# The opening stage of a two-layer diffusion transformer step: token array loaded first, one modulation chunk in halves, constants moved in the queue, dummy products added

## The reference

```
m = silu(cond) @ w_ada + b_ada           -> shift1, scale1, gate1, shift2, scale2, gate2
h = rms_norm(x, g_mix) * (1 + scale1) + shift1
q, k, v, gb, gc, xin = split(h @ w_in)   # k, q of the latent tokens get rotary positions (cos, sin)
x = x + gate1 * (concat(diff_attention(q, k, v), gb * short_conv(gc * xin)) @ w_out)
h = rms_norm(x, g_ffn) * (1 + scale2) + shift2
x = x + gate2 * ffn(h)                   # layer 0: SwiGLU; layer 1: the best 2 of 8 experts
```

## Time and profile before

| | |
|---|---|
| median of 3 runs | 2062.04 us (2062.03 to 2066.11) |
| the profiled execution | 2062.37 us |
| its span, first to last instruction | 2060.6 us |
| mean granted TensorE clock | 0.962 |
| busy: PE, DVE, ACT, POOL | 93%, 52%, 39%, 6% |

### The profile page before, as it was taken

The page is one execution under the profiler, slowest core; times in us unless marked ns, Lnnn a source line. Parts: engine busy times, 40 slices in busy tenths (PEclk is TensorE's granted clock), DMA queues, the critical chain, the costliest instruction groups (busy, mean ns, idle before and its releaser), DMA issues. The chain is left out here.

```text
span 2060.6 us, 29699 instructions
## 1 busy us (share of the span) xinstructions
PE 1915.9 (93%) x12189; PEld 1737.4 (84%) x12189; DVE 1067.3 (52%) x1661; ACT 799.6 (39%) x1278; POOL 113.4 (6%) x93
## 2 busy tenths in 40 slices
PE   4699988999999999989999898699999999999795
PEld 2699957989999999989997687689898898988784
DVE  1542576443232322336326754577686676866574
ACT  3321155242211222233213643455565565655552
POOL 2000000100000000110000001020000000002201
PEclk7899999989999999989999999799999999999997
DMA  8314300322322242304251010467666676668551
GB/s 318 133 72 184 122 12 1 123 93 93 133 72 103 108 168 72 113 31 159 88 199 58 1 42 33 169 218 232 216 225 223 218 231 218 221 225 296 172 174 52
DMA packets 84813, 289.53 MB, mean 141 GB/s; under 512 B 10660, under 2 KB 14116, under 8 KB 84672
## 3 DMA queue, kind: packets, MB, share of 16 engines
q1 hardware_dynamic: 78192, 270.14, 37.7%
q0 software_dynamic: 6480, 17.43, 2.5%
HBM read 281.12 MB, written 12.26 MB: 142 GB/s over the span
## 5 line engine op out<-in xcount | busy, mean ns | idle before, releaser
L1502 DVE TENSOR_TENSOR w_lo<-raw,w_hi 128x1024 fp32r<-128x1024 f32 x396 | 490.7, 1241 | 433.0 <-ACT w_hi L1084 419.7
L1084 ACT ACTIVATE w_hi<-raw 128x1024 fp32r<-128x1024 f32 x396 | 417.6, 1055 | 377.6 <-PE ps L615 179.3
L615 PE MATMUL ps<-a_hi,w_hi 128*128 128x320 f32 x1728 | 402.6, 315 | 32.6 <-DVE w_lo L1502 15.9
L615 PE MATMUL ps<-a_lo,w_hi 128*128 128x320 f32 x1728 | 397.5, 312 | 0.0
L615 PE MATMUL ps<-a_hi,w_lo 128*128 128x320 f32 x1728 | 397.3, 311 | 0.0
L928 PE MATMUL ps<-hg,w_hi 128*128 128x416 f32 x1232 | 384.5, 370 | 12.8 <-DVE w_lo L1502 10.7
L615 PEld LDWEIGHTS ps<-a_hi,w_hi 128*128 128x128 f32 x1728 | 291.5, 191 | 50.6 <-issue 30.6
L929 PE MATMUL ps<-hg,w_lo 128*128 128x208 f32 x1232 | 317.4, 258 | 0.0
L615 PEld LDWEIGHTS ps<-a_lo,w_hi 128*128 128x128 f32 x1728 | 292.6, 190 | 0.0
L615 PEld LDWEIGHTS ps<-a_hi,w_lo 128*128 128x128 f32 x1728 | 292.4, 190 | 0.0
L928 PEld LDWEIGHTS ps<-hg,w_hi 128*128 128x128 f32 x1232 | 234.3, 190 | 15.3 <-DVE w_lo L1502 11.2
(11 more groups left out here) (212 smaller groups left out, 2039.2 us busy)
## 6 DMA issues: line engine op xcount, KB each, us to landing
raw<-gu_w SPq DMA_DIRECT2D x222, 512.0 KB
raw<-moe_down_w SPq DMA_DIRECT2D x88, 512.0 KB
ada_raw<-ada_w SPq DMA_DIRECT2D x21, 2048.0 KB, 8.0
raw<-in_w SPq DMA_DIRECT2D x48, 512.0 KB
raw<-down_w SPq DMA_DIRECT2D x22, 512.0 KB
raw<-out_w SPq DMA_DIRECT2D x16, 512.0 KB
ada_pro<-ada_w SPq DMA_DIRECT2D x3, 2048.0 KB, 17.5
y_rows<-ey POOLq DMA_DIRECT2D x7, 512.0 KB, 3.6
```

Source lines behind the costliest of these rows:

```text
L615: ins = nc.tensor.matmul(out[:, hf, 0:HALF], w, o[:, hf * HALF:(hf + 1) * HALF], start=f, stop=e)
L1084: nc.scalar.activation(w_hi[:, s, :], raw[:, n % RAW, :], ACT.Copy).then_inc(hi_done, 1)
L1502: nc.vector.tensor_tensor(w_lo[:, s, :], raw[:, n % RAW, :], w_hi[:, s, :].bitcast(F32), ALU.subtract)\
```

## The change

ADA_FIRST and the blocks are written in another order, KEEP_BUSY gives a number of dummy products ahead of each item, the loads are issued in another order, the last opening chunk comes in two halves of columns with a semaphore each, DVE's wait for the late constants moves to the first rotary step, and the lambda sums and token numbers move behind chunk v0, with a semaphore of their own for lam_qk.

```diff
-ADA_FIRST = [("rows", 0, 0), ("rows", 0, 1), ("rows", 1, 0), ("turn", 0, 0), ("norm", 0, 0), ("rows", 1, 1),
-             ("spread", 0, 0), ("turn", 1, 0)]
+ADA_FIRST = [("rows", 0, 0), ("norm", 0, 0), ("rows", 0, 1), ("spread", 0, 0), ("rows", 1, 0), ("turn", 0, 0),
+             ("rows", 1, 1), ("turn", 1, 0)]
+KEEP_BUSY = {("rows", 0, 0): 40, ("norm", 0, 0): 4, ("rows", 0, 1): 2, ("spread", 0, 0): 0, ("rows", 1, 0): 8,
+             ("turn", 0, 0): 0, ("rows", 1, 1): 2, ("turn", 1, 0): 2}
             # SP
-            sp.dma_start(ada_raw[:], quad(0, 0, 0)).then_inc(ada_full, 16)
             for dst, src in ((bada, b_ada), (idn, ident), (gmix, g_mix)):
                 sp.dma_start(dst[:], src).then_inc(consts_in, 16)
             for kb in range(KB):
                 sp.dma_start(x[:, kb, :], xT[:, kb, :]).then_inc(x_in[kb], 16)
-                if kb == KB // 2 - 1:
-                    sp.dma_start(ada_pro[:, 0], quad(0, 0, 1)).then_inc(pro_full[0], 16)
-            for q in range(2):
-                sp.dma_start(ada_pro[:, 1 + q], quad(0, 1, q)).then_inc(pro_full[1 + q], 16)
+            sp.dma_start(ada_raw[:], quad(0, 0, 0)).then_inc(ada_full, 16)
+            sp.dma_start(ada_pro[:, 0], quad(0, 0, 1)).then_inc(pro_full[0], 16)
+            sp.dma_start(ada_pro[:, 1], quad(0, 1, 0)).then_inc(pro_full[1], 16)
+            for hf in range(2):
+                cols = slice(512 * hf, 512 * (hf + 1))
+                sp.dma_start(ada_pro[:, 2, :, cols], quad(0, 1, 1)[:, :, cols]).then_inc(pro_full[2 + hf], 16)
...
                 for item, c in IN_ITEMS[l][0]:
+                    if c == 2 and l == 0:
+                        for dst, src in late:
+                            sp.dma_start(dst[:], src).then_inc(late_in, 16)
                     if c == RAW:
                         if l == 0:
                             sp.wait_ge(mm_done, ROWS_FIRST[-1] + 1)
-                            for dst, src in late:
-                                sp.dma_start(dst[:], src).then_inc(late_in, 16)
+                            sp.dma_start(lq, lam_qk.partition_broadcast(P)).then_inc(lam_in, 16)
             # PE
+            def keep_busy(g, count):
+                for _ in range(count):
+                    nc.tensor.matmul(ps[:, g % 4, 1, 0:P], ones[:], ones[:], start=True, stop=True)
...
                 for hf in range(2):
+                    if arrived:
+                        pe.wait_ge(arrived[hf], 16)
                     for j in range(QUAD):
...
+                    if arrived and hf == 0:
+                        ins.then_inc(half_rows, 1)
             # ACT
                     for kb in range(KB):
-                        if kb == KB // 2:
-                            act.wait_ge(mm_done, ROWS_FIRST[1] + 1)
-                            take_rows(0, g0)
                         square(0, kb)
                     root(0, D)
+                    act.wait_ge(mm_done, ROWS_FIRST[1] + 1)
+                    take_rows(0, g0)
+                    act.wait_ge(mm_done, q0 + ADA_FIRST.index(("turn", 0, 0)) + 1)
+                    act.wait_ge(half_rows, 1)
+                    take_half_rows(1, g0, 0)
                     act.wait_ge(mm_done, ROWS_FIRST[3] + 1)
-                    act.wait_ge(mm_done, q0 + ADA_FIRST.index(("turn", 0, 0)) + 1)
-                    take_rows(1, g0)
+                    take_half_rows(1, g0, 1)
             # DVE
+                    reciprocal_root(0)
                     dve.wait_ge(row_done, 1)
                     dve.sem_inc(blk_free, 1)
                     modulation(l, 0, g0 + ADA_BLOCK["turn", 0], q0 + ADA_FIRST.index(("turn", 0, 0)))
-                    reciprocal_root(0)
-                    dve.wait_ge(row_done, 2)
-                    dve.sem_inc(blk_free, 1)
-                    modulation(l, 1, g0 + ADA_BLOCK["turn", 1], q0 + ADA_FIRST.index(("turn", 1, 0)))
-                    split_lo(0)
-                    split_lo(1)
-                norm(2 * l, operand[l, "h1"])
-                if l == 0:
-                    dve.wait_ge(late_in, 16 * 10)
-                    for each in range(LAYERS):
-                        lambda_sums(each)
-                    token_numbers()
+                    def first_gains():
+                        dve.wait_ge(row_done, 3)
+                        dve.sem_inc(blk_free, 1)
+                        split_lo(0)
+                        modulation(0, 1, AT[0, "ada"][2] + ADA_BLOCK["turn", 1],
+                                   AT[0, "ada"][1] + ADA_FIRST.index(("turn", 1, 0)), 1)
+                        split_lo(1)
+                norm(2 * l, operand[l, "h1"], first_gains if l == 0 else None)   # called behind the second st
...
+                        if (l, kind, j) == (0, "k", 0):
+                            dve.wait_ge(late_in, 16 * 9)
...
                         dve.wait_ge(vt_ready, 4 * l + j + 1)
                         dve.sem_inc(blk_free, 1)
+                        if l == 0 and j == 0:
+                            dve.wait_ge(lam_in, 16)
+                            for each in range(LAYERS):
+                                lambda_sums(each)
+                            token_numbers()
```

More of the change, by code:

```diff
@@ L118 @@
     LO_BASE.append(LO_BASE[-1] + 2 + FB + (ST if _e == LAST_E else 0))
-ADA_FIRST = [("rows", 0, 0), ("rows", 0, 1), ("rows", 1, 0), ("turn", 0, 0), ("norm", 0, 0), ("rows", 1, 1),
-             ("spread", 0, 0), ("turn", 1, 0)]
-ADA_BLOCK = {("rows", 0): 0, ("rows", 1): 1, ("turn", 0): 2, ("turn", 1): 3, ("norm", 0): 4, ("spread", 0): 4}
+ADA_FIRST = [("rows", 0, 0), ("norm", 0, 0), ("rows", 0, 1), ("spread", 0, 0), ("rows", 1, 0), ("turn", 0, 0),
+             ("rows", 1, 1), ("turn", 1, 0)]
+ADA_BLOCK = {("rows", 0): 1, ("rows", 1): 2, ("turn", 0): 3, ("turn", 1): 3, ("norm", 0): 4, ("spread", 0): 4}
 QUAD = 4
+KEEP_BUSY = {("rows", 0, 0): 40, ("norm", 0, 0): 4, ("rows", 0, 1): 2, ("spread", 0, 0): 0, ("rows", 1, 0): 8,
+             ("turn", 0, 0): 0, ("rows", 1, 1): 2, ("turn", 1, 0): 2}
 def mingle(items, groups, allowed):
@@ L394, in hybrid_step @@
         ada_full = sem("ada_full")
-        pro_full = [sem(f"pro_full{i}") for i in range(3)]
+        pro_full = [sem(f"pro_full{i}") for i in range(4)]
         cs_ready = sem("cs_ready")
@@ L646, in norm_sums @@
                 n0, q0, g0 = NORM_AT[i]
-                open_block(g0)
+                if i:
+                    open_block(g0)
                 pe.wait_ge(ss_add, KB * (i + 1))
@@ L653, in norm_spread, with weigh_conditions @@
                 spread(NORM_AT[i][2], diag[:].rearrange("p t c -> p (t c)"))
-            def weigh_conditions(src, g, q, first, last):
+            def weigh_conditions(src, g, q, first, last, arrived=()):
                 for hf in range(2):
+                    if arrived:
+                        pe.wait_ge(arrived[hf], 16)
                     for j in range(QUAD):
@@ L667, in turn_rows @@
                 for j in range(KB):
-                    ins = nc.tensor.matmul(ps[:, g % 4, 0, 2 * j:2 * j + 2], mrow[:, j * P:(j + 1) * P], fold[:],
+                    if halves and j == KB // 2:
+                        pe.wait_ge(row_done, count + 1)
+                    ins = nc.tensor.matmul(ps[:, g % 4, int(halves), 2 * j:2 * j + 2], mrow[:, j * P:(j + 1) * P], fold[:],
                                            start=True, stop=True)
@@ L692, in _ @@
                     for kind, grp, q in ADA_FIRST:
+                        spread_done = (kind, grp, q) in ADA_FIRST[ADA_FIRST.index(("spread", 0, 0)) + 1:]
+                        keep_busy(g0 + ADA_BLOCK["turn" if spread_done else "norm", 0], KEEP_BUSY[kind, grp, q])
                         g = g0 + ADA_BLOCK[kind, grp]
@@ L696, in _ @@
                             weigh_conditions(ada_raw, g, q, True, False)
+                        elif (kind, grp, q) == ("rows", 1, 1):
+                            weigh_conditions(ada_pro[:, 2], g, q, False, True, pro_full[2:])
                         elif kind == "rows":
@@ L719, in _ @@
                         if item[1] == "turn":
-                            turn_rows(g0 + b, item[2] + 1)
+                            turn_rows(g0 + b, item[2] + 2)
                         else:
@@ L851, in _ @@
                             if item[1] == "turn":
-                                turn_rows(g, item[2] + 1)
+                                turn_rows(g, item[2] + 2)
                             else:
@@ L1127, in take_rows, with take_half_rows @@
                                      ps[:, (g0 + ADA_BLOCK["rows", grp]) % 4, :, :], ACT.Copy).then_inc(row_done, 1)
+            def take_half_rows(grp, g0, hf):
+                nc.scalar.activation(mrow[:, 512 * hf:512 * (hf + 1)],
+                                     ps[:, (g0 + ADA_BLOCK["rows", grp]) % 4, hf, :], ACT.Copy).then_inc(row_done, 1)
             act.wait_ge(cond_in, 16)
@@ L1519, in halves, with norm @@
                 return a.rearrange("p (a b) -> p a b", a=2)
```

(4 more changed lines are left out.)

14 lines of the change are left out of this document (8 added, 6 removed).

## The result

The changed kernel took 2043.35 us (median of 4 runs, 2041.94 to 2047.64) against 2064.07 us (4 runs, 2062.03 to 2066.69) of the kernel before: ratio 0.9901, 95% interval 0.9885 to 0.9917, so 20.7 us faster. The profiled execution took 2042.01 us, 20.4 less than that of before. Forecast were 26.2 less for it and 2036.0 for the median, with 2041.5 as the range's upper end: the direction and the gain at k2 are right, the gain in the opening is half of what was forecast.

What follows compares the result with a forecast made beforehand. The prediction took PE, busy 93%, as the bound, with time to give only where it idles or slows: 2062.37 (profiled) - 15.9 - 2.4 - 7.9 = 2036.2, median 0.3 lower, so 2036.0 us; range 2032.5 to 2041.5.

Steps and rivals of the forecast that it cites:

- The stall, 15.9 + 2.4 = 18.3: At k2: PE's 15.9 us wait for w_lo goes, and 2.4 us of half clock after that idle time.
- their cover: Constants land near 42.5 us, needed about 57; the 2.6 us of lambda sums fit beside a v chunk of 7.0.
- The opening, 7.9: Up to PE's first input product: it comes at 41.1 us instead of 48.96, a gain of 7.9 us.
- PE, at full clock: In the opening: PE's items run at full clock, a chunk 1.92 us, ten sums 2.2, a turn 1.9.
- half clock in parts of the fill: Rival in the opening: some items run at half clock, 3.5 to 7 us lost, 2039.5 to 2043; chance 0.25.
- 40 dummies end near 16: Before chunk 1: dummies from 3.0 us, 0.28 each at full clock, end near 16, before the landing at 17.3.
- the sum's 5 us at half clock: At the opening's start: the first 5 us of dummies run at half clock, 0.46 us each, then at full clock.
- The plug: Rival in the opening: 58 dummies block PE at half clock throughout, 2059.4 to 2085 us; chance 0.02.
- The second assumption: In the opening: with turn and sums standing between chunks and dummies, the clock was expected to stay full.
- the law: Opening loads: landing is bytes at 406 GB/s plus a constant of 5.4 us; first 17.3, last half 32.8.
- Bias first: Behind the last turn (37.2 us): w_lo 0 ends at 37.6, bias and gains at 38.1, first product at 41.1.
- Within 4 us is no change: Whole kernel: a change under 0.2% (4 us) counts as none, as three runs spread that much; chance 0.02.

Runs made afterwards that it cites:

- e1: The kernel before with only the constants' part of the change (early constants, lambda sums behind v0), opening as before: 2046.02 us, ratio 0.9916.
- e5: The changed kernel with 54 dummies ahead of the first chunk instead of 40, and none of the 18 later ones: 2040.51 us, ratio 0.9876.
- e4: The changed kernel with 54 dummies ahead of the first chunk instead of 40, the 18 later ones kept: 2041.46 us, ratio 0.9885.
- e12: e5 with the last opening chunk loaded as one transfer instead of two halves: 2042.15 us, ratio 0.9888.
- e10: e5 with DVE's bias and gains made ahead of w_lo 0 and w_lo 1: 2042.81 us, ratio 0.9892.
- e11: e10 with 13 more dummies between the last turn and the first product: 2036.81 us, ratio 0.9874.
- a2: The changed kernel run again with nothing edited: 2044.75 us, ratio 0.9898.
- e1b: A repeat of e1, one trace: 2042.76 us.

## Why the prediction was partly right

- **The stall, 15.9 + 2.4 = 18.3:** right, 17.9 here and 18.1 in e1. Constants and lambda sums found their cover: no wait appears for either, and the sums stand at 117.8, beside v.
- **The opening, 7.9: this failed, in the step "PE, at full clock".** It gave 3.95, as the rival "half clock in parts of the fill" had it, by the same items that this rival priced. By the starts of the items, measured against forecast: chunk 1 0.4 later (landing); then +1.7 (chunk 1 at 3.64), +0.8 (four dummies partly at half clock), +1.1 (chunk 2 at 3.07), +0.5 (spread), -0.3 (eight dummies in 1.88, not 2.2): about 4.1 late at chunk 3 (32.52 for 28.4), and 3.9 late at the first product (45.01 for 41.1). What stands behind chunk 3's start is as forecast, 12.5 us for 12.7, DVE's new order with it.
- **"40 dummies end near 16" was the term that began it.** They ended at 13.6. A dummy, two passes, cost 0.22 us at full clock and not 0.28, and 0.43 at half clock and not 0.46 (the passes of 2.90 to 13.40). With these prices and the sum's 5 us at half clock they would have ended near 14.2; the half clock lasted 3.2 us instead, which makes up the rest. (In e5, by its 14.80 us for 54, it lasted longer.) Idle time of 4.1 us before chunk 1 followed. The plug never threatened: most of the first 40 ran at the full level.
- **The second assumption failed too:** that dummies between narrow items keep the clock. e4 and e5 show chunk 2 slow either way.
- **A weight load and the dummies.** The Trainium skill (TensorE: Matmul & The Clock Gate, Part 3) would have a dummy pay its load in full. A pass of the spread took 0.54 us at half clock (four from 38.35 to 40.51), which is 0.22 when scaled from its 320 columns to 128; a dummy's pass took 0.21 at that level (15 in 3.20 us), so the load added nothing: the trace does not agree.
- **Landings:** the law was 0.4 us too early for the first one and 1.5 for the last (34.3 in e5, for 32.8). The queue still moved 405 GB/s, so the rate was right; 0.8 of the additional 1.1 us lie between the first and the second (6.0 us in e5, where 2.1 MB at 406 GB/s are 5.2), and their cause is not known. That a chunk in halves lands later than a whole one, as the figure for 1 MB in the Trainium skill (DMA: Bandwidth & Descriptors, Bandwidth) would have had it, e5 and e12 do not show (34.29 and 34.27).
- **Bias first:** the sum let DVE's w_lo 0 stand ahead of the bias and gave 3.9 us from the last turn to the first product, which is what came (3.97). e10, with the bias first, took 3.70.
- **The range:** it ended at 2041.5 while the rival that came true was priced at 2039.5 to 2043, with 1.5 us more lost behind v0. "Within 4 us is no change" was taken from three runs and was narrow for single runs: those of the kernel before spread from 2058.19 to 2067.92 over all its runs here.

## What to carry to other kernels

When a late wait is removed, look at what stands behind it on every engine: here one 17.6 us wait for a small constant held PE for 15.9 us and cost it the clock as well, and that part of the forecast held to 0.4 us. Where two gains stand one behind the other, split them at a milestone between them: here DVE's new order gave its 3.1 us, and only the fill fell short. Dummy products belong only where PE would be idle anyway, and their number has to be right at its end: just up to a landing (e5) or just up to the first product (e11), and the landing itself moves (17.73 to 18.91 us in the traces here); ahead of ready work they cost their time and here saved nothing. Before trusting a clock in a row, check it against the time of a known item: ahead of a trace's first record it prints as 1.00. Judge a change of a few microseconds by milestones in the trace near it, since what is behind them varied by 11 us in this kernel with nothing changed there.

## What the runs showed of the chip that was not expected

- Half clock followed stretches in which PE was busy without a gap, but with ten sums of one column: 21.4 to 26.0 in the changed kernel has PE busy for 4.60 of 4.60 us and a clock of 0.81, and chunk 2 behind it 0.60. Yet 30.3 to 37.0, with a turn of products two columns wide among the chunks, kept 1.00. Being busy by the records and keeping the clock are two things.
- The clock's falls in an unchanged program differ between executions: the same place at 0.50 in a2 and at 1.00 in the first trace, 17 us of half-clock time between them, 6.3 us of time. The Trainium skill (TensorE: Matmul & The Clock Gate, Part 1) says that the point at which a kernel's clock first rises is different from run to run, and puts what the rise costs at under 1% of a typical span. The traces agree: by the passes of the first dummies the rise came at 6.1 us in the changed kernel, 3.2 us of half clock in 2040. The falls behind it cost more: 102.0 to 133.0 us at half clock behind v0, at 0.34 us each.
- Yet some patterns were stable: the old opening came to its first product at 48.64 to 49.15 in three traces of before, and at 51.46 and 51.08 in the traces of e1 and e1b, whose code on PE is the same until then. In before the clock rose at 30.1, for the first turn; in e1 30.0 to 42.2 is all at 0.50. What makes it rise 12 us later there is open.
